# Merge with ten buffers of logits and two for output weights, in memory that the normalised rows give back

## What is computed

```python
def merge(h, branches, pgate):
    silu_gates = jnp.split(jax.nn.silu(pgate), N_BRANCH, -1)
    acc = None
    for i in range(N_BRANCH):
        term = jax.nn.sigmoid(h @ w_gate[l, i]) * ((branches[i] * silu_gates[i]) @ w_branch[l, i])
        acc = term if acc is None else acc + term
    return acc @ w_out[l]
...
x_new = layer_norm(DEEPNORM_ALPHA * x + gt_x * out_x) * ln_g[l] + ln_b[l]
```

## Time and profile before

| what | value |
|---|---|
| median of 3 runs | 4112.87 us (4107.26 to 4117.56) |
| the profiled execution, its own time | 4113.7 us |
| its span, first to last instruction | 4111.9 us |
| TensorE busy | 83% |
| DVE, ACT, POOL busy | 46%, 27%, 26% |
| mean granted TensorE clock | 0.923 |
| merge of layer 0, first to last matmul | about 1885.5 to 2043.1 us |
| merge of layer 1, first to last matmul | about 3883.1 to 3996.5 us |

### The profile page before, as it was taken

One profiled execution on the slowest core, in us unless ns is written; L12 is line 12 of the kernel. 1 busy time (PEld: TensorE's weight loads), 2 busy tenths in 40 slices (PEclk: granted clock), 3 DMA queues, 4 the chain that ended last, 5 costly groups with the idle time before them and its releaser, 6 DMA issues. The chain is left out here.

```text
span 4111.9 us, 62489 instructions
## 1 busy us (share of the span) xinstructions
PE 3416.2 (83%) x25372; PEld 2696.2 (66%) x25372; DVE 1907.8 (46%) x2999; ACT 1100.1 (27%) x1926; POOL 1088.4 (26%) x1156
## 2 busy tenths in 40 slices
PE   5988988578979888996794989988679878988678
PEld 3875567366767776885682776666567656766557
DVE  5214542694365554114465214532882645553256
ACT  2002321483222121213312102321661321211341
POOL 2011101441134442223502013002440334442250
PEclk8988999699989999998897989999899989999889
DMA  5011002211122111435644111014101121112573
GB/s 230 1 50 48 7 33 84 67 27 62 32 63 66 51 58 53 130 115 171 206 155 197 41 47 63 7 38 112 43 25 64 51 80 50 60 53 83 163 235 132
DMA packets 200978, 334.38 MB, mean 81 GB/s; under 512 B 23424, under 2 KB 96896, under 8 KB 196992
## 3 DMA queue, kind: packets, MB, share of 16 engines
q1 hardware_dynamic: 171904, 283.34, 21.6%
q10 hardware_dynamic: 28800, 47.20, 3.1%
HBM read 249.45 MB, written 81.00 MB: 80 GB/s over the span
## 5 line engine op out<-in xcount | busy, mean ns | idle before, releaser
L89 PE MATMUL ps<-hh,wh_ds 128*128 128x512 f32 (+1 forms) x1600 | 670.2, 419 | 143.9 <-PEq L78 88.4
L90 PE MATMUL ps<-hl,wh_ds 128*128 128x512 f32 (+1 forms) x1600 | 611.8, 382 | 0.0
L91 PE MATMUL ps<-hh,wl_ds 128*128 128x512 f32 (+1 forms) x1600 | 610.4, 382 | 0.0
L89 PEld LDWEIGHTS ps<-hh,wh_ds 128*128 128x128 f32 x1600 | 318.2, 199 | 234.6 <-issue 118.4
L196 POOL CAST wh_ds<-raw_ds 128x512 fp32r<-128x512 f32 x160 | 104.5, 653 | 1151.8 <-POOLq L78 614.6
L90 PEld LDWEIGHTS ps<-hl,wh_ds 128*128 128x128 f32 x1600 | 319.2, 200 | 57.2 <-issue 13.9
L91 PEld LDWEIGHTS ps<-hh,wl_ds 128*128 128x128 f32 x1600 | 317.4, 198 | 56.0
L183 ACT ACTIVATE out_ds<-ps 128x512 f32<-128x512 f32 (+1 forms) x200 | 110.2, 551 | 537.3 <-PE ps L91 482.2
L1083 DVE TENSOR_REDUCE nmx_d<-ps 128x1 f32<-128x1280 f32 (+1 forms) x144 | 193.9, 1366 | 39.7 <-PE ps L1012 39.5
L89 PE MATMUL ps<-yh_mg,wh_ds 128*128 128x256 f32 (+1 forms) x320 | 132.9, 415 | 95.5 <-DVE wl_ds L2278 95.5
L198 POOL TENSOR_TENSOR wl_ds<-raw_ds,wh_ds 128x512 fp32r<-128x512 f32 x160 | 208.7, 1305 | 12.8
(11 more groups left out here) (320 smaller groups left out, 7505.8 us busy)
## 6 DMA issues: line engine op xcount, KB each, us to landing
gate_sums<-out_ds ACTq DMA_DIRECT2D x160, 256.0 KB, 2.0
raw_ds<-in_d_wmerge SPq DMA_DIRECT2D x128, 256.0 KB, 2.7
logit_mg<-gate_sums SPq DMA_DIRECT2D x128, 256.0 KB, 3.6
w_mr<-in_d_wmod SPq DMA_DIRECT2D x16, 1536.0 KB, 10.0
R_dr<-decay_rows SPq DMA_DIRECT2D x80, 256.0 KB, 4.4
qk_da<-turned_qk SPq DMA_DIRECT2D x32, 320.0 KB, 7.8
q_raw_da<-turned_qk SPq DMA_DIRECT2D x288, 32.0 KB, 1.8
acc_ou<-merged SPq DMA_DIRECT2D x18, 512.0 KB, 4.7
```

What stands on the lines that cost most here:

```text
L89: pe.matmul(out, w_hi, x_hi, start=first, stop=False)
L90: pe.matmul(out, w_hi, x_lo, start=False, stop=False)
L91: return pe.matmul(out, w_lo, x_hi, start=False, stop=last)
```

## The change

`hh` and `hl` are now allocated for each layer, on the right side of SBUF, and given back inside `merge` after `apply_gates`. In that memory the output weights get tensors of their own, which live until `output` has ended. With the space that is left:

- the logits get ten buffers in place of four;
- `wo` gets two buffers with a semaphore each in place of one; a piece waits for the one before the last;
- SP loads the weights of block f + 1 right behind the first logits of block f, no more behind the store at b == 2; at the start the weights of block 1 go behind the first logits, no more ahead of them;
- ACT and DVE cut the weights of block f + 1 after the last chunk of b == 1 of block f, no more after the last chunk of b == 2 (ACT) and the first of b == 3 (DVE).

The number of matmuls, multiplications, additions, cuts and DMAs, and the bytes of each, stay as they were.

```diff
-def merge(nc, m, l):
+def merge(nc, m, l, rows, weights):
...
-        LOGITS, TERMS = 4, 2
+        LOGITS, TERMS = 10, 2
+        rows.close()
+        m.wo = [weights.enter_context(nc.sbuf_tensor(f"w_out_{n}{l}", [P, KD, D], F32R, side="right")) for n in ("high", "low")]
+        wo_h, wo_l = m.wo
...
-        wo = sb("wo", [P, 512])
+        wo = sb("wo", [P, 2, 512])
...
                 weights(0)
-                weights(1)
                 for u, (f, b, n) in enumerate(products):
                     at, width = chunks[n]
                     if u >= LOGITS:
...
                     if out_piece(u):
                         i, k, part = out_piece(u)
-                        if i:
-                            sp.wait_ge(wo_low, i)
-                        sp.dma_start(wo[:], m.d_wout[l, k, :, part]).then_inc(wo_in, 16)
+                        if i >= 2:
+                            sp.wait_ge(wo_low, i - 1)
+                        sp.dma_start(wo[:, i % 2], m.d_wout[l, k, :, part]).then_inc(wo_in[i % 2], 16)
+                    if b == 0 and n == 0 and f + 1 < KD:
+                        weights(f + 1)
                     if b == 2 and n == 0 and f >= 1:
                         sp.wait_ge(added, 3 * n_c * f)
                         sp.dma_start(m.d_acc[:, f - 1, lo:], acc[:, (f - 1) % 2, lo:]).then_inc(stored[(f - 1) % 2], 16)
-                        if f + 1 < KD:
-                            weights(f + 1)
...
-                        act.wait_ge(wo_in, 16 * (i + 1))
-                        act.activation(m.hh[:, k, part], wo[:], ACT.Copy).then_inc(wo_high, 1)
-                    if b == 2 and n == n_c - 1 and f + 1 < KD:
+                        act.wait_ge(wo_in[i % 2], 16 * (i // 2 + 1))
+                        act.activation(wo_h[:, k, part], wo[:, i % 2], ACT.Copy).then_inc(wo_high, 1)
+                    if b == 1 and n == n_c - 1 and f + 1 < KD:
                         cut(f + 1)
...
-                        dve.tensor_tensor(m.hl[:, k, part], wo[:], m.hh[:, k, part].bitcast(F32), ALU.subtract
+                        dve.tensor_tensor(wo_l[:, k, part], wo[:, i % 2], wo_h[:, k, part].bitcast(F32), ALU.subtract
                                           ).then_inc(wo_low, 1)
-                    if b == 3 and n == 0 and f + 1 < KD:
+                    if b == 1 and n == n_c - 1 and f + 1 < KD:
                         cut(f + 1)
...
-    wo_h, wo_l = m.hh[:, :, 0:D], m.hl[:, :, 0:D]
+    wo_h, wo_l = m.wo
...
-        m.hh = sb("hh", [P, KD, ROWS], F32R)
-        m.hl = sb("hl", [P, KD, ROWS], F32R)
...
         for l in range(DEPTH):
+            weights = st.enter_context(ExitStack())
             with ExitStack() as layer:
+                rows = layer.enter_context(ExitStack())
+                m.hh, m.hl = (rows.enter_context(nc.sbuf_tensor(f"{n}{l}", [P, KD, ROWS], F32R, side="right"))
+                              for n in ("hh", "hl"))
...
-                merge(nc, m, l)
+                merge(nc, m, l, rows, weights)
                 m.dense.free()
             output(nc, m, l, out)
+            weights.close()
```

More of the change, by code:

```diff
@@ L2190, in merge @@
         names = [f"logit_in{s}" for s in range(LOGITS)]
-        wo = sb("wo", [P, 512])
+        wo = sb("wo", [P, 2, 512])
         with phase(nc, "w_in", "w_high", "w_low", "sigm", "branched", "multiplied", "added", "stored0", "stored1",
-                   "wo_in", "wo_high", "wo_low", *names) as (
-                block, w_in, w_high, w_low, sigm, branched, multiplied, added, stored0, stored1, wo_in, wo_high, wo_low,
+                   "wo_in0", "wo_in1", "wo_high", "wo_low", *names) as (
+                block, w_in, w_high, w_low, sigm, branched, multiplied, added, stored0, stored1, wo_in0, wo_in1, wo_high, wo_low,
                 *logit_in):
-            stored = [stored0, stored1]
+            stored, wo_in = [stored0, stored1], [wo_in0, wo_in1]
             products = [(f, b, n) for f in range(KD) for b in range(4) for n in range(n_c)]
```

## The result

| kernel | median us (range) | ratio to before, 95% | profiled execution, span | mean clock |
|---|---|---|---|---|
| before | 4112.49 (4107.26 to 4117.56) | | 4113.7, 4111.9 | 0.923 |
| changed | 4058.42 (4053.84 to 4061.38) | 0.9878 [0.9866, 0.9891] | 4053.8, 4052.0 | 0.925 |

The change is worth 54.1 us, where 59.7 were forecast. Measured a second time it was 4054.79 beside 4103.65, 0.9868 [0.9846, 0.9890], or 48.9 us.

A forecast was written before the change was run, and what follows sets the result against it. TensorE was taken to bound the kernel, held in both merges by late weight cuts and a lowered clock. Savings of 43.1 and 17.6 us, less 1, gave 59.7; 4112.9 - 59.7 = 4053 us, range 4044 to 4076.

The forecast's parts named there:

- The earlier cut: Both merges: cutting the next block's weights earlier removes TensorE's waits, 25.4 and 14.7 us, and slow clock, 19.9 and 7.2.
- The period of layer 0: Layer 0 merge: time per block 14.1 us, between 13.8 and 14.6; merge 114.5 us, saving 43.1.
- a bubble: Merges: DMA gaps at the two stops in the queue may add half a microsecond.
- The loop through the store: Merges: added, store, logits landing, sigmoid, multiplication, remaining adds; 12.5 to 14.2 us in layer 0, 11.0 to 12.7 in layer 1.
- Layer 1: Layer 1 merge: time per block 11.6 us, between 11.1 and 12.7; merge 95.8 us, saving 17.6.
- The stops in SP's queue: Merge loads: the weights' wait for the cut costs nothing while six products, 6.9 us, outlast one landing, 5.75.
- The sign given for the loop: Merges: ACT waits for logits once a block, behind the store, and POOL has almost no idle time in layer 1.
- a DMA share of 0.95: Both merges: ten logits buffers keep DMA almost always busy, with shares near 0.95.
- the slow clock: Rival, merges: TensorE's clock still falls, so only the waits go, 25.4 + 14.7 us; 4074 us, chance 0.07.
- DMA gave more than now: Against the rival that ten buffers fetch no faster than 244 GB/s in the merges; 4095 us, chance 0.07.
- Same instructions, same bytes: nothing: Second output-weight buffer, new places, rows given back: gap and output stage keep their steps; 1 us of loss taken.

The follow-up runs named there:

- two_products: Changed kernel with the second of each product's three merge matmuls left out; merges 101.1 us in layer 0 and 88.0 in layer 1.
- act_store: Changed kernel with the store of a merged block issued from ACT's queue in place of SP's; 4054.22 us, ratio 0.9862 to before.
- two_act: Changed kernel with each product's second merge matmul left out and the store issued by ACT; merges 96.0 us in layer 0, 88.8 in layer 1.
- after_again: Changed kernel measured and profiled once more, nothing edited; 4054.79 us beside 4103.65 for before, ratio 0.9868.
- right: Kernel before with only hh and hl put on the right side of SBUF for the whole program; 4119.11 us beside 4111.59, ratio 1.0017.
- place: Changed kernel's new memory places alone, with four logits buffers, one output-weight piece, old loads and cuts; 4118.17 us beside 4110.97 for before, ratio 1.0010.
- the second pair: Kernel before and changed kernel, both unedited, profiled again; merges with gaps 61.6 us shorter, medians 48.9 us apart.

## Why the prediction was right, and which step was mis-sized

It was right: 4058.4 lies in 4044 to 4076, 5.4 us above the 4053 forecast. Two errors in it partly cancel: the merges saved 44.7 + 19.9 = 64.6 us where 43.1 + 17.6 = 60.7 were forecast, and a term that was put at nothing cost more than that.

**The earlier cut**: right. Of 25.4 and 14.7 us of waits, 0 and 2.2 are left. The clock came back with them: 0.98 and 0.96, and 1.00 for 88 us on end. That the cut takes 1.74 us "wherever it sits" was not: the rows below show 1.22 in layer 0 and up to 2.32 in layer 1.

**The period of layer 0**: 14.1 forecast. DVE's cuts of the changed kernel (start us, us; the counterpart of the earlier trace rows), three of layer 0 and three of layer 1:

```profile
1912.13 1.22 DVE L2280 TENSOR_TENSOR wl_ds<-w_mg,wh_ds 128x1024 fp32r<-128x1024 f32 x1
...
1953.65 1.22 DVE L2280 TENSOR_TENSOR wl_ds<-w_mg,wh_ds 128x1024 fp32r<-128x1024 f32 x1
...
1981.33 1.22 DVE L2280 TENSOR_TENSOR wl_ds<-w_mg,wh_ds 128x1024 fp32r<-128x1024 f32 x1
...
3852.09 1.21 DVE L2280 TENSOR_TENSOR wl_ds<-w_mg,wh_ds 128x1024 fp32r<-128x1024 f32 x1
...
3909.74 2.29 DVE L2280 TENSOR_TENSOR wl_ds<-w_mg,wh_ds 128x1024 fp32r<-128x1024 f32 x1
...
3920.74 2.32 DVE L2280 TENSOR_TENSOR wl_ds<-w_mg,wh_ds 128x1024 fp32r<-128x1024 f32 x1
```

(1981.33 - 1912.13) / 5 = 13.84 us, TensorE's own 13.8. The 0.3 us that were added for a bubble didn't come, and the merge saved 157.6 - 112.9 = 44.7 in place of 43.1.

**The loop through the store**: right in size in layer 0, where it is about 13.06 us as soon as TensorE needs less (two_products), some 0.8 below TensorE. So it is indeed next, but hidden. For layer 1 it was given as late next too; there act_store and two_act show that it isn't the bound.

**Layer 1**: 11.6 forecast, (3920.74 - 3852.09) / 6 = 11.44 measured; 19.9 us saved in place of 17.6. It is TensorE's own 11.1 but for the start and one late cut: after_again needs 91.8 us, where the prediction's 88.5 for eight blocks and 3.0 for the slow first microseconds make 91.5. The wait of 2.02 at 3912.09 has a slow stretch behind it, from about 3913.65 to 3917.00; the wait of 0.18 at 3898.90 has none.

**The stops in SP's queue**: right, they cost nothing, though they are 30.5 + 14.3 us in layer 0. The sign given for the loop, POOL almost without idle time in layer 1, didn't show: it is busy for 64.09 of 94 us. Nor did a DMA share of 0.95: it is 0.87, and 0.91 in the middle of layer 0.

**The rivals**: the slow clock didn't stay, and DMA gave more than now (296 and 299 GB/s, where 208 and 244 were the earlier trace rows). The Trainium skill, "TensorE: Matmul & The Clock Gate", section "A second HAM failure mode: psum-queue depth-cycling", spoke for a clock that keeps swinging. This trace doesn't agree: with all eight banks cycled, 459 matmuls ran in 88.00 us at 1.00.

**The step that failed**: "Same instructions, same bytes: nothing", for which 1 us was booked. The gaps behind the merges did hold (13.66 for 15.11). But the new place of the rows costs 7.5 us (2.9 to 11.5) by right, in stages that weren't in the sum at all; place, with the change's own places, has the same sign, 7.2 us by its medians, but an interval that takes in zero. The working went stage by stage through what the change touches; tiles that move are read in other stages too. With the merges and gaps as measured (65.6) and this term (7.5) the sum is 58.1, against 54.1 measured; what is left, 4.0 us (in the second pair, 61.6 - 7.5 - 48.9 = 5.2), isn't explained. The wander of the untouched stages (3804.5 to 3811.3 in the same kernel) is of that size.

## What to carry to other kernels

Cut or prepare what the next block needs in the middle of this one, and give the loads enough buffers to pass the queue's stops: either half alone left a merge at 125 to 127 us, both together brought it to TensorE's own 113, and six buffers did as much as ten. Once a stage runs at an engine's own pace, more buffers or a better queue win nothing; a part left out on that engine shows what is next and how far off. When tiles are given a new place, time the new place by itself, and count every stage that reads them.

## What the runs showed of the hardware

- The pace of matmuls isn't one number, even with nothing waited for, clock 1.00 and one form, 128x512: in the output stage of layer 0 it is 226.7 ns in before and 228.9 in right, where only tiles have moved. Which tile's place does it isn't told apart, and the place isn't the whole of it: act_store, with all tiles where the changed kernel has them, fits 302 into 70 us of layer 1's output stage, after_again 308.
- DVE and POOL hold each other up. POOL's adds on the changed kernel's timeline:

```profile
1952.46 1.30 POOL L2317 TENSOR_TENSOR dv<-dv,raw_ds 128x512 f32<-128x512 f32 x1 [0.53 <-DVE raw_ds L2296]
1953.82 2.21 POOL L2317 TENSOR_TENSOR dv<-dv,out_ds 128x512 f32<-128x512 f32 x1
...
3909.23 1.72 POOL L2317 TENSOR_TENSOR dv<-dv,raw_ds 128x512 f32<-128x512 f32 x1
```

  The add at 1953.82 began just behind the cut at 1953.65 and took 2.21 us for 1.30; in layer 1 the cut that began at 3909.74 came behind an add that ran from 3909.23 to 3910.95, and took 2.29 for 1.21. It ended at 3912.03, and TensorE's wait of 2.02 at 3912.09 with it. The Trainium skill, "SBUF — State Buffer", section "Who interferes with whom", says that a DVE instruction with two inputs in SBUF and a GpSimd instruction that reads SBUF lock each other out, whichever starts first; these rows agree.
- The 16 DMA engines carried 338 GB/s at a share of 0.98, most of it loads of 256 KB through ten buffers of logits (two_act, layer 0); with four such buffers the merge, with all its matmuls, got 208 before and 254 with the new order.
